# One eighth fewer block products for sa, a twelve-chunk branch loop, and eight of the 31 taps formed on ScalarE and summed by DMA

## What is computed

```python
hn = rms_norm(h, norm_g)                      # h: 16 meta tokens + 512 tokens
z = einsum("btd,dn->btn", hn, w_in)           # 2048 -> 7 * 2048
xa, sa, vb, gb, sb, ma, mb = split(z)
ya = causal_depthwise_conv(xa, conv_a_w, conv_a_b)            # 4 taps
ya = rg_lru(ya, w_rg, b_rg, w_ig, b_ig, lru_lambda)           # two 128x128 gates per head, scan over tokens
pa = (ya * silu(sa)) @ w_proj_a
yb = causal_depthwise_conv(vb * sigmoid(gb), conv_b_w, conv_b_b)   # 31 taps
pb = (silu(layer_norm(yb)) * silu(sb)) @ w_proj_b
h = h + (sigmoid(ma) * pa + sigmoid(mb) * pb) @ w_out
out = rms_norm(h, final_g)[:, 16:]
```

## Time and profile before

| | before |
|---|---|
| median of three runs | 1796.1 us (1795.7 to 1797.14) |
| the profiled execution | 1798.06 us, span 1796.5 us |
| busy: PE, PE weight load, DVE, ACT, POOL | 99%, 93%, 72%, 40%, 10% |
| mean granted TensorE clock | 0.996 of full |
| chain that ended last: PE, DVE, the rest | 93%, 3%, 4% |

### The profile page before, as it was taken

The page is one execution under the profiler, slowest core; times in us unless marked ns, Lnnn a source line. Parts: engine busy times, 40 slices in busy tenths (PEclk is TensorE's granted clock), DMA queues, the critical chain, the costliest instruction groups (busy, mean ns, idle before and its releaser), DMA issues.

```text
span 1796.5 us, 30396 instructions
## 1 busy us (share of the span) xinstructions
PE 1772.9 (99%) x12308; PEld 1662.0 (93%) x12308; DVE 1290.4 (72%) x1600; ACT 719.7 (40%) x960; POOL 178.8 (10%) x196
## 2 busy tenths in 40 slices
PE   9899999999999999999999999999999999999998
PEld 8799999999999999998999999999888899997886
DVE  7969797979888888889777766788623387663431
ACT  6543324242424242332555555555423154443322
POOL 0500000000000000000112111122100111111000
PEclk9999999999999999999999999999999999999999
DMA  6233333333333333344877756676667688848422
GB/s 205 64 107 95 112 93 107 101 107 94 110 93 105 100 93 111 93 135 135 223 223 201 220 155 180 158 203 182 235 216 234 175 215 199 194 132 269 153 82 94
DMA packets 217127, 269.68 MB, mean 150 GB/s; under 512 B 7504, under 2 KB 187856, under 8 KB 215888
## 3 DMA queue, kind: packets, MB, share of 16 engines
q1 hardware_dynamic: 168240, 188.21, 32.6%
q0 software_dynamic: 48800, 80.23, 18.2%
HBM read 227.52 MB, written 40.89 MB: 149 GB/s over the span
## 4 chain that ended last, share of the span: by engine, by line
PE 93%; DVE 3%; issue 2%; DMA 1%; ACT 1%; POOL 0%; SPq 0%; DVEq 0%; ACTq 0%; POOLq 0%
PE psum L687 52%; PE psum L724 30%; PE psum L879 6%; PE psum L893 2%; PE psum L784 1%; DMA t_lo<-m_spill 1%; DMA raw<-in_w_proj_a 1%; DVE region L1733 0%; DMA region<-in_x_channels 0%; DVE region L1370 0%; DVE t_lo L1652 0%; DVE w_lo L1294 0%; DVE total L1420 0%; DVE c_lo L1385 0%; POOL t_lo L603 0%
## 5 line engine op out<-in xcount | busy, mean ns | idle before, releaser
L687 PE MATMUL psum<-x_hi,w_hi 128*128 128x264 f32 (+1 forms) x1888 | 452.8, 306 | 7.5 <-ACT w_hi L908 3.0
L687 PE MATMUL psum<-x_lo,w_hi 128*128 128x264 f32 (+1 forms) x1888 | 452.4, 306 | 0.0
L687 PEld LDWEIGHTS psum<-x_hi,w_hi 128*128 128x128 f32 x1888 | 306.7, 189 | 23.2 <-ACT w_hi L908 3.5
L1316 DVE SCALAR_TENSOR_TENSOR region<-region,conv_cols 128x512 f32<-128x512 f32 x480 | 326.8, 747 | 0.0
L687 PEld LDWEIGHTS psum<-x_lo,w_hi 128*128 128x128 f32 x1888 | 306.4, 189 | 14.9 <-issue 0.2
L908 ACT ACTIVATE w_hi<-raw 128x1024 fp32r<-128x1024 f32 x128 | 135.6, 1059 | 437.4 <-PE psum L687 399.5
L687 PE MATMUL psum<-x_hi,w_lo 128*128 128x264 f32 (+1 forms) x1888 | 290.9, 304 | 0.0
L687 PEld LDWEIGHTS psum<-x_hi,w_lo 128*128 128x128 f32 x1888 | 260.2, 188 | 14.9
L1294 DVE TENSOR_TENSOR w_lo<-raw,w_hi 128x1024 fp32r<-128x1024 f32 x128 | 158.2, 1236 | 59.8 <-ACT w_hi L908 59.7
L1536 DVE TENSOR_TENSOR w_lo<-region,w_hi 128x1024 fp32r<-128x1024 f32 x87 | 106.5, 1224 | 85.5 <-ACT w_hi L1079 85.3
L1536 DVE TENSOR_TENSOR x_lo<-region,x_hi 128x1024 fp32r<-128x1024 f32 x87 | 106.3, 1223 | 69.4 <-ACT x_hi L1079 67.9
(11 more groups left out here) (226 smaller groups left out, 3206.8 us busy)
## 6 DMA issues: line engine op xcount, KB each, us to landing
raw<-in_w_in SPq DMA_DIRECT2D x140, 512.0 KB, 3.5
region<-in_w_in SPq DMA_DIRECT2D x42, 1024.0 KB, 6.5
region<-in_w_proj_b SPq DMA_DIRECT2D x16, 1024.0 KB, 7.5
raw<-in_w_out SPq DMA_DIRECT2D x32, 512.0 KB, 4.0
raw<-in_w_proj_a SPq DMA_DIRECT2D x31, 512.0 KB, 3.5
region<-in_w_in POOLq DMA_DIRECT2D x21, 512.0 KB, 6.4
sigmoid_spill<-wide POOLq DMA_DIRECT2D x16, 512.0 KB, 5.3
aux<-conv_b_spill POOLq DMA_DIRECT2D x16, 512.0 KB, 5.7
```

Source lines behind the costliest of these rows:

```text
L687: last = pe.matmul(psum[:, bank, 0:width], weights[:, s, k, m * P:(m + 1) * P], operand[part][:, place(4 * group + k), t0:t0 + width], sta ...
L1316: ins = dve.scalar_tensor_tensor(conv_b[:, t, :], moved, w, conv_b[:, t, :], ALU.mult, ALU.add)
```

## The change

The projection `sa` leaves the branch loop and joins stage 3: NX goes from 21 to 28. Plain pairs of ma go from three to four, of which the first takes the place of sa in `first_body`. What the loop used to multiply by silu(sa) at once (`h`, the scan's result) is spilled as it is, loaded again by POOL in the sa units (`load_h`), and multiplied there (`gate_ya`, one DVE instruction a unit).

The branch loop has twelve chunks (`ITEMS_BODY`), written out seven times in place of a hardware loop. A chunk now holds one tile of 128 channels and half of the contraction, in the order xa, xa, gb, gb, vb, vb by tile, so that each tile is finished after two chunks; the loads have rows of 512 bytes in place of 1024. The gate rounds stand before chunks 4 to 7 (counted from 0).

Of the 31 taps of conv_b DVE keeps 23. For the other eight ACT writes the first into `conv_by_act` (`first_tap`) and seven products (`tap_product`) into two alternating buffers that belong to `decay` and `sig_gb`; POOL adds each to `conv_by_act` by an accumulating DMA inside SBUF (`add_taps`), one for each of the two tiles, and DVE adds the sum at the end (`join_conv`). The first tap of conv_a is ACT's too. The layer norm's total is summed by accumulating DMAs (`sum_conv`) and not by DVE. The copies of parameter columns are gone.

In `first_body` the matmul of the mean stands between the `hi` and the `lo` passes of the fifth chunk, and the seventh chunk is cut by ACT and DVE ahead of the scaling of x.

```diff
         LO_BY_DVE = 3
-        STD = 3
-        NX = 3 * PAIRS - STD
+        STD = 4
+        NX = 4 * PAIRS - STD
         NV = NX + PAIRS
-        C0 = PAIRS * BODY
-        W0 = C0 + 4 * STD
+        C0 = BODY + (PAIRS - 1) * ITEMS_BODY
+        W0 = C0 + 4 * (STD - 1)
         A0 = W0 + 7 * NX
         B0 = A0 + 4 * PAIRS
         O0 = B0 + 7 * PAIRS
-        MA, MB, SB, PA, PB = range(5)
+        MA, MB, SA, SB, PA, PB = range(6)
+        ACT_TAPS = 8
+        STEPS_AT = {1: (0,), 2: (1,), 3: (2, 3), 4: (4,), 5: (5,), 6: (6,)}
         A11, S1, S2, A12, S3, A22, S4 = range(7)
...
-            with sp.Fori(1, PAIRS) as i:
-                branch_body(i)
+            body(0, [c for col in (COL_XA, COL_MA, COL_GB, COL_VB) for c in columns(w_in_v, col)], x_too=True)
+            for i in range(1, PAIRS):
+                for p in range(ITEMS_BODY):
+                    n, half = item_chunk(i, p), p % 2
+                    column = (COL_XA, COL_GB, COL_VB)[p // 4] + 256 * i + P * (p // 2 % 2)
+                    sp.wait_ge(lo_ready, n + 1 - RING)
+                    sp.dma_start(raw[:, n % RING, :].rearrange("p (k n) -> p k n", n=P),
+                                 w_in_v[:, KH * half:KH * (half + 1), column:column + P])\
+                        .then_inc(raw_loaded[n % RING], 16)
...
+            def sum_conv(i):
+                for j in (2 * i - 2, 2 * i - 1):
+                    wait(pool, conv_summed, 16 * j)
+                    pool.dma_start(total[:, :], conv_b[:, j % 2, :], accum_op=ALU.add).then_inc(conv_summed, 16)
...
+            def add_taps(i, s):
+                n = (ACT_TAPS - 1) * (i - 1) + s
+                for t in range(2):
+                    if s == 0:
+                        pool.wait_ge(conv_begun, 2 * i - 1 + t)
+                    wait(pool, tap_added[t], 16 * n)
+                    pool.wait_ge(tap_ready[t], n + 1)
+                    pool.dma_start(conv_by_act[:, t, :], products_at(s + 1, t), accum_op=ALU.add)\
+                        .then_inc(tap_added[t], 16)
...
-                spill_ya(i + -1)
-                spill_conv(i)
-            spill_ya(PAIRS - 1)
+                spill_h(i - 1)
+                if i > 1:
+                    spill_conv(i - 1)
+                    sum_conv(i - 1)
+                for step in range(ACT_TAPS - 1):
+                    add_taps(i, step)
+            spill_h(PAIRS - 1)
...
                 passes(w_hi_v, (0, 1))
+                if mean:
+                    pe.wait_ge(x_summed, CT - 1)
+                    pe.matmul(psum[:, 7, :], average[:, :], total[:, :], start=True, stop=True).then_inc(x_mean, 1)
                 pe.wait_ge(lo_ready, plus(n, 1))
...
+            def item(i, p):
+                n, half, bank = item_chunk(i, p), p % 2, 2 * (p // 2 % 3)
+                hi, lo = (w[:, n % RING, :].rearrange("p (k n) -> p k n", n=P) for w in (w_hi, w_lo))
+                def passes(weights, parts):
+                    for k in range(KH):
+                        for part in parts:
+                            for h in range(2):
+                                last = pe.matmul(
+                                    psum[:, bank + h, 0:HALF], weights[:, k, :],
+                                    part[:, KH * half + k, h * HALF:(h + 1) * HALF],
+                                    start=half == 0 and k == 0 and weights is hi and part is x_hi,
+                                    stop=half == 1 and k == KH - 1 and weights is lo)
+                    return last
...
+            def branch_body(i):
+                for p in range(ITEMS_BODY):
+                    if p == 0:
+                        pe.wait_ge(gb_sigmoid, 2 * i)
+                    elif p == 2:
+                        pe.wait_ge(vb_gated, 2 * i - 1)
+                    elif p == 4:
+                        pe.wait_ge(vb_gated, 2 * i)
+                        pe.wait_ge(gate_hi_ready, i + 1)
+                        pe.wait_ge(gate_lo_ready, i + 1)
+                    elif p == 6:
+                        pe.wait_ge(xa_copied, 2 * i + 1)
+                    elif p == 8:
+                        pe.wait_ge(xa_copied, 2 * i + 2)
+                    elif p == 10:
+                        pe.wait_ge(gb_sigmoid, 2 * i + 1)
+                    if 4 <= p < 8:
+                        gate_round(i, p - 4)
+                    item(i, p)
...
+                cut_hi(0, 6)
                 norm_tiles_hi(5)
-                cut_hi(0, 6)
                 norm_tiles_hi(6)
                 cut_hi(0, 7)
                 cut_gates_hi(0)
...
+            def xa_copy(i, t):
+                act.wait_ge(multiplied, item_chunk(i, 2 * t + 1) + 1)
+                act.wait_ge(h_spilled, 16 * i)
+                act.activation(xa_pad[:, t, 4:].rearrange("p (h n) -> p h n", h=2),
+                               psum[:, 2 * t:2 * t + 2, 0:HALF], ACT.Copy).then_inc(xa_copied, 1)
+                act.wait_ge(xa_copied, 2 * i + t + 1)
+                j = 2 * i + t
+                act.activation(conv_a[:, t, :], xa_pad[:, t, 4 - (KA - 1):4 - (KA - 1) + T], ACT.Identity,
+                               scale=params[:, j, CONV_A_W:CONV_A_W + 1], bias=params[:, j, CONV_A_B:CONV_A_B + 1])\
+                    .then_inc(conv_a_begun, 1)
...
+            def tap_product(i, s):
+                n, k = (ACT_TAPS - 1) * (i - 1) + s, s + 1
+                for t in range(2):
+                    j = 2 * i - 2 + t
+                    if s == 0:
+                        act.wait_ge(h_ready, 2 * i)
+                    elif s == 1:
+                        act.wait_ge(vb_gated, 2 * i)
+                    else:
+                        act.wait_ge(tap_added[t], 16 * (n - 1))
+                    act.activation(products_at(k, t), yb_pad[:, t, META + k:META + k + SEQ], ACT.Copy,
+                                   scale=params[:, j, CONV_B_W + k:CONV_B_W + k + 1]).then_inc(tap_ready[t], 1)
...
             def branch_body(i):
-                for p in range(12):
-                    cut_hi(i, p)
+                for p in range(ITEMS_BODY):
+                    chunk_hi(item_chunk(i, p))
+                    if p == 1:
+                        t_hi_of(i - 1)
+                        first_tap(i)
                     if p == 2:
-                        t_hi_of(i + -1)
+                        xa_copy(i, 0)
                     if p == 3:
                         cut_gates_hi(i)
-                    if p == 5:
-                        group_done(i, 4)
-                        act.wait_ge(ya_ready, 2 * i)
-                        for t in range(2):
-                            act.activation(xa_pad[:, t, 4:].rearrange("p (h n) -> p h n", h=2),
-                                           psum[:, 2 * t:2 * t + 2, 0:HALF], ACT.Copy).then_inc(xa_copied, 1)
-                    if p >= 8:
-                        cut_c_hi(i, p - 8)
+                    if p == 4:
+                        cut_c_hi(i, 0)
+                        xa_copy(i, 1)
+                    for step in STEPS_AT.get(p, ()):
+                        tap_product(i, step)
+                    if 5 <= p < 9:
+                        read_gates(i, p - 5)
+                    if 5 <= p < 8:
+                        cut_c_hi(i, p - 4)
+                    if p == 7:
+                        act.wait_ge(multiplied, item_chunk(i, 5) + 1)
+                        act.wait_ge(tap_added[0], 16 * ((ACT_TAPS - 1) * (i - 1) + ACT_TAPS - 2))
+                        gb_sigmoid_of(0, 4)
+                    if p == 8:
+                        v = decay_of(i)
...
+            TAPS = [0, 3, 3, 1, 2, 1, 3, 3, 3, 2, 2, 0]
...
+            def join_conv(i, before):
+                for t in range(2):
+                    dve.wait_ge(tap_added[t], 16 * (ACT_TAPS - 1) * i)
+                    steps.done(before[t])
+                    dve.tensor_tensor(conv_b[:, t, :], conv_b[:, t, :], conv_by_act[:, t, :], ALU.add)\
+                        .then_inc(conv_b_done, 1)
...
+                cut_lo(0, 6)
                 norm_tiles(5)
-                cut_lo(0, 6)
                 norm_tiles(6)
                 unscaled_xa()
                 cut_lo(0, 7)
...
-                for p in range(12):
-                    cut_lo(i, p)
+                for p in range(ITEMS_BODY):
+                    chunk_lo(item_chunk(i, p))
                     if p == 0:
-                        one_step(dve.tensor_copy(conv_cols[:, :, :], lru_cols[:, :, :]))
-                        dve.wait_ge(root_ready, 2 * i)
-                        one_step(dve.tensor_copy(lru_cols[:, :, :], params[:, ds(2 * i, 2), :]))
-                        t_sums(i + -1)
+                        t_sums(i - 1)
+                    if p == 3:
+                        t_lo_of(i - 1)
+                        conv_a_taps(i, range(1, KA), (0,), conv)
                     if p == 4:
                         cut_gates_lo(i)
-                    if p in (5, 6):
```

(19 more changed lines are left out.)

445 lines of the change are left out of this document (239 added, 206 removed).

## The result

The changed kernel takes 1800.9 us (median of 10 runs, 1796.1 to 1805.2) against 1795.9 us before (10 runs beside them). The ratio is 1.0026, with a 95% interval of 1.0016 to 1.0036: 5 us **slower**, not 10 us faster. It is the prediction's second rival, the late adds, that came.

The account below looks back on a forecast made before the run. PE, busy 99% of the span, was taken to set the time wherever it doesn't wait. PE's work −15.4, first body −3.1 and new waits +8.5 sum to −10.0 us: 1796.1 to 1786 us, range 1776 to 1802.

Parts of the forecast that it names:

- second rival: In the loop, adds landing late (L = 6.1) delay the second gate round 6.1 us a turn: 1820; chance 0.20.
- PE's work: Seven sa pairs move from loop chunks to block-product units, 22.13 to 19.93 us each: 15.4 us less.
- rival 1: The loop's new wait before the second gate round is hidden: 1777.6 us; chance 0.22.
- The first body: Before the loop, earlier mean and seventh-chunk cuts bring the gate round forward: 3.1 us less, between 1.8 and 4.7.
- The half clock: First body, behind the wait at 78.13: 3.00 us at 0.50 clock, costing 1.5; gone only in the 4.7 case.
- The ladder: Chained ACT and DVE steps from chunk 3's end to c_lo: PE waits 1.2 us a turn, 8.5 us more.
- rung: One step of that chain before the second gate round; the three conv_a taps were 2.30 of its 7.8 us.
- The DMA chain: In the loop, products wait for adds two steps before, delaying the second gate round to 6.1 + 3L: no cost forecast.
- L: Issue to landing of the second tile's add: taken as 4.0 to 4.5 us, free up to 4.07.
- The prediction's own rule: In the loop, L hides up to 4.5 us; from there each microsecond costs three in a turn.
- Loads with rows of 512 bytes, gate_ya, the total's adds: Loop loads landing in 6.4 us fit 6.5 of room; gate_ya fits its unit; total's adds land in time: no cost.
- rival 3: The clock falls at every new wait in the loop, seven times 1.5 us: 1797, no change; chance 0.06.

Follow-up runs that it names:

- e11: Changed kernel with one step of products a chunk, c_lo ahead of the three conv_a taps, and `t_lo_of` in chunk 2, two buffers: 1779.9 us.
- e7: Changed kernel with its two first-body edits undone (mean's matmul and seventh chunk's cuts back in their old places): 1804.0 us.
- e3: Changed kernel plus a third pair of product buffers, with `t_lo_of` moved from chunk 3 to chunk 2: 1786.1 us.
- e5: e3 plus c_lo for the second gate round cut ahead of the three conv_a taps: 1780.7 us.
- e1: Changed kernel without POOL's fourteen adds of tap products a turn; ACT still makes the products: 1788.4 us.
- e9: Changed kernel with every add of a tap product made a plain copy of the same 256 KB, same order and waits: 1786.1 us.
- e2: Changed kernel with DVE cutting c_lo for the second gate round ahead of the three conv_a taps: 1800.4 us.
- e10: Changed kernel with the seven steps of tap products spread one to a chunk over chunks 1 to 7: 1787.5 us.
- e8: Changed kernel without products or adds; ACT keeps only its first tap and DVE does 30 taps in place of 23: 1824.2 us.

## Why the prediction was wrong, by its own steps

- **PE's work, −15.4 us: right.** Units of 19.93 us where sa is. With a loop almost without waits the kernel takes 1779.9 (e11), and rival 1, in which the new wait is hidden, had 1777.6.
- **The first body, −3.1 us: right.** The two edits together are worth 3.1 us in the medians and 3.2 in the traces (e7); no run took them apart. The first body ended 4.9 sooner, but 1.3 of that stood there before the first edited instruction (the last sum of x, 36.52 against 37.80). The half clock behind the first gate round stayed.
- **The ladder, one wait of 1.2 us before the second gate round: right, but not what set the time.** It stands in e3 as 1.10 us in six of seven turns (0.74 in the first), and goes with one rung (e5). Where `t_lo_of` is still in chunk 3, it is less and has a partner that I did not have: 0.43 us before the first round and 0.44 before the second (e1, e9). In the changed kernel late adds lay over it, so removing the rung there did nothing (e2). The sum that I gave, 1786, is e3's 1786.1; as e3 also moves `t_lo_of`, the match to 0.1 us is luck in part. (7 × 1.2 is 8.4 and not 8.5, of no account here.)
- **The DMA chain: the term that failed.** I took L for 4.0 to 4.5 us, from a plain 256 KB row plus half of what accumulation adds to 512 KB, and called it free. L was 4.9 in the median, 6.4 at most. The prediction's own rule, 3 us a turn for each us above 4.5, gives 1.2 + 3 × 0.4 = 2.4 us a turn at 4.9, and the trace has 18.1 / 7 = 2.6: mis-sized by half a microsecond, at a place with a slope of three, seven times. The chain is as I drew it: in the turn shown the last product of step 1 is out at 278.44 + 1.32 = 279.76, and the add of step 3 has landed by 295.28, 15.5 us later, which is 0.6 + 3 × 4.97. With plain copies of 3.3 us the cost was gone (e9), with adds of 4.9 us spaced for it also (e3, e10). Of the 14.9 us between 1786 and 1800.9 the waits are 18.1 − 8.5 = 9.6, the half clock 1.7 and the wait in the ma pairs 1.6; the other 2 have no row.
- **How L was mis-sized.** The bounds, 2.7 and 6.1, held the value; the point taken between them did not. The plain part was 3.3 here and not 2.7 (e9), and accumulation added 1.6 and not 1.3. Part of that was a slip of mine: the 2.6 us that I halved took the quickest accumulating row, 5.8, from the median of the plain ones, 3.2; with the median, 6.1, half is 1.45.
- **A path that the chain did not have.** I followed the late product only to the second gate round. The product of step 3 stands in chunk 3 ahead of the cut of chunk 4, and made the first round late too: 8.8 of the 18.1 us, of which the 3.1 that e1 keeps are DVE's order. The sum of both waits came out near my single one because PE, held at the first round, comes as much later to the second; that is my reading, and no run separates the two.
- **Loads with rows of 512 bytes, gate_ya, the total's adds: at no cost, but for one.** The loads of the loop land in 4.3 us in the median (before 3.5) and nothing in the loop waits for them. The total's adds take 4.3 us. Behind the loop DVE waits 2.77 us for one of them at 654.49, ahead of the `w_lo` that PE then waits 1.6 us for, at 658.00; of that I had nothing.

```profile
654.49 1.00 DVE L1455 TENSOR_SCALAR region<-region,params 128x512 f32<-128x512 f32 x2 [2.77 <-DMA total<-region]
...
656.73 1.22 DVE L1676 TENSOR_TENSOR w_lo<-raw,w_hi 128x1024 fp32r<-128x1024 f32 x1
```

- **The clock.** The forecast's rival 3 did not come: behind 13 of the 14 waits the granted clock stayed at the 2.4 GHz level, behind the longest, 2.01 us at 374.07, it fell for some 3.5 us (1.7 us lost). The stretches behind that one:

```profile
374.00:378.00 4.00, 3.93 (x20) 3.96 (x21) 2.43 (x3) 2.10 (x4) 1.52 (x2) 0.57 0.36 65
378.00:384.00 6.00, 6.00 (x52) 6.00 (x51) 4.80 (x8) 2.33 (x6) 1.55 (x3) 1.00 0.98 204
```

The Trainium skill ("TensorE: Matmul & The Clock Gate", HAM oscillation — how this bites in real kernels) has a kernel go cold in every tile that waits, with waits of some 3 to 5 us in its drawing. The six waits of 4.4 to 4.8 us in e8 agree with it. The waits of the changed loop, 0.7 to 2.0 us, are shorter than those of that kernel, and thirteen in fourteen did not do it, so my use of it against this change went too far.

## What to carry to other kernels

A transfer that a buffer waits for has no price of its own: its price is what stands behind the wait on that engine, so look there first, and put nothing urgent behind an instruction that waits for a DMA. When a cost is free up to a limit and steep behind it, and your estimate ends within half a microsecond of the limit, the forecast is the steep side as much as the flat one; spacing the work (one step a chunk, worth 13.4 us here) asks for no better estimate. And an order edit that is worth nothing may be worth 5 us once the wait that covers it is gone, so try it again then.
